# A two-layer transformer kernel: the opening on a turned copy of x, token-form first gates with the norm's root applied late, and the last block's last unit in two column halves

## The chip, the cores and the metric

One core of one Trainium2 chip. The metric is the device time of one launch in microseconds, lower is better; the number compared is the median of several runs.

## The reference

Batch 1, 256 tokens, model width 1024, all fp32. Two stacks of two layers each run one after the other. What matters here is the very first sub-block and the very last one:

```python
h = x                                                   # 256 x 1024
h = h + 0.5 * swiglu(rmsnorm(h, ffn1_norm[0]), w_gate, w_up, w_down)   # D_FF = 2816
# rmsnorm(x, g) = x * rsqrt(mean(x*x) + 1e-6) * g ;  swiglu = (silu(u @ w_gate) * (u @ w_up)) @ w_down
u = rmsnorm(h, mix_norm[0]);  z = u @ w_in[0]           # the mixer: attention, pooling, gates ...
...                                                     # the rest of both stacks
# second stack, last layer: r = ALPHA * h + relu(h @ w_ff1)**2 @ w_ff2 ; out = layer_norm(r, ln2_g, ln2_b)
```

The root of an RMS norm is one number per token, the gain one number per column of x. So (x * root * g) @ W equals root * ((x * g) @ W), row by row.

## The kernel before, in words

**Products.** Every weight comes from HBM once, as a *unit* of at most 128x2048 fp32 (1 MB), into one of six buffers `raw` (NL = 6). ScalarE (ACT) copies it to a rounded high part `wh` (`high`, five buffers, NH = 5), VectorE (DVE) subtracts to get a low part `wl` (`low`). Activations are split the same way into `xh`/`xl` (slots X, 8 column blocks of 128) or `mh`/`ml` (slots M, 12). A product is three matmuls per block: low weight, high weight, and low activation with high weight.

- *Token form* (`group`, item `tokens`, L1529): the activation is stationary, 512 (or fewer) weight columns move. A unit is visited once for each 128 tokens, t = 0 and 1. The result has tokens on the partitions and must be turned (four 128x128 transposes on TensorE (PE), L1552, then ACT high and DVE low) before the down product can use it.
- *Wide form* (`wide_group`, item `wide`, L1540 and L1543): the weight is stationary, 8 matmuls of 512 and 8 of 256 columns for each 128 of a unit's 256 columns. The result is already turned; DVE adds its halves (`wadd`).

**The plan.** `Plan` writes one list of items, once, before any instruction exists; each engine's program walks it and issues its own part, so the list's order is each engine's queue order. After each visit (or each half of a wide group) `tick` runs: deferred items, then `pump`, then `advance`, which places `fetch` of unit j once unit j-6 is used up, and `high` of j once j-5 is (`low` of j follows at the next `advance`). `pump` resumes the head generator of each of four lanes once. A lane is a first-in first-out queue: what is appended to it starts only when the generator ahead has ended.

Lane 0 first holds `opening`. In the kernel before its first statements place the rest of the norm and the turning of x, `consts` comes at pump 8, and then `tables` follows:

```python
def tables(self):
    for _ in range(40):
        yield
    for i in range(10):
        self.add("table", i=i)
        yield
```

That is: table 0 at pump 48, table 9 at pump 57, lane 0 free from pump 58. After a sub-block's last down units, `after(t, b)` places the squares, at b = 1 also the norm (`rms`), and appends a generator for turning the normed h of these 128 tokens into slots X: to lane 0 for t = 0, to lane 3 for t = 1. It yields WAIT_RMS = 2 times and then places both turns. If a product finds its slots not ready, `need` pumps until the turn is placed, and then goes on with the product behind it.

**Layer 0, `ffn1`.** 2816 columns in two rounds, (512, 512, 512) and (512, 512, 256). The first 512 are in token form: gate in units of 2 blocks, up in units of 4 (6 units). All others are in wide form, 256 columns at a time. Each round ends with `down`: 6 units, then 5 (one, and four visited first all by t = 0, then all by t = 1, `end=True`). That makes 12 + 16 + 12 + 20 + 10 = 70 ticks; the last visit of t = 0 is followed by pump 66, that of t = 1 by pump 70. The mixer's first group starts with four visits of t = 0.

**The opening.** SP issues x of t = 0, two units, x of t = 1, then more units. PE runs filling matmuls (`wake`) and spreads the gain row over the partitions through PSUM (`spread`, L1563, waits for a 4 KB DMA issued by ACT). For t = 0: squares on ACT, root on GpSimd (POOL, power of -0.5), norm on DVE into `xn`, turn, split; then product; the rest and t = 1 are placed between the first visits. `held` keeps `advance` from placing splits meanwhile.

**The end.** The last `down` group visits four units (two 512-deep weight halves times two column halves b) by t = 0, then by t = 1. Per column half: `hadd` (L2026), `bn_stats` (L2041); after b = 1 `bn_aggr`, then POOL adds epsilon and takes the power (L1433, L1436) while DVE does (h - mean) * g (L2049), DVE finishes (L2055), SP stores.

Of the kernel before, what the change touches and what calls it, by code (L numbers as in the profile page):

```python
# [3 lines left out]

# [4 lines left out]
F32 = mybir.dt.float32  # L9
# [10 lines left out]
L = 2  # L20
# [46 lines left out]
class Memory:  # L67


    def __init__(self, nc, A, out, ctx):  # L70
# [20 lines left out]
        self.fill_set, self.first_set = s("fill_set"), s("first_set")  # L91
        self.rows_set, self.row_landed = s("rows_set"), s("row_landed")
# [28 lines left out]
                      "weights_ready": self.weights_ready, "y_low": self.y_low}  # L121
# [11 lines left out]
    def sbuf(self):  # L133
# [36 lines left out]
        self.lam = A("lam", take(8), [P, 2])  # L170
        self.bn = A("bn", take(128), [P, 2, 16])
# [21 lines left out]
        self.gain_rows = A("gain_rows", o_g[0], [P, D])  # L193
        self.fill = A("fill", o_g[0] + 4096, [P, 512], F32R)
        self.first = A("first", o_g[0] + 6144, [P, P])
# [164 lines left out]
class Plan:  # L360
# [5 lines left out]
    def __init__(self, total):  # L366
# [9 lines left out]
        self.held = False  # L376
# [119 lines left out]
    def group(self, jobs, start=False, end=False):  # L496

        idx = [self.take(j["key"]) for j in jobs]
        for t, u in self.visits(len(jobs), start, end):
# [8 lines left out]
            v = self.pe("tokens", j=j, t=t, X=X, slots=slots, segs=segs, first=job["first"], stop=job["last"], need=need)  # L508
# [7 lines left out]
            if job["last"]:  # L516
                job["epi"](t, v["p"], [u[0] for u in segs])
# [35 lines left out]
    def once_open(self, go):  # L553

        def gen():
            while self.held:
                yield
            for _ in range(8):
                yield
            go()  # L560
        if self.held:
            self.lanes[3].append(gen())
        else:
            go()
# [7 lines left out]
    def rms(self, t, gain, final=False, halves=(0, 1)):  # L572
        n = self.next("normed", 2)
        self.add("rms", t=t, gain=gain, final=final, sq=self.count["squared"], n=n, c=self.next("rstd"), halves=halves,
                 spread=self.spread if gain == 0 else None)
# [5 lines left out]
    def rms_rest(self, t, gain):  # L581
        self.add("rms", t=t, gain=gain, final=False, c=self.count["rstd"] - 1, halves=(1,),
                 spread=self.spread)
# [28 lines left out]
    def to_ln(self, gname, bname, l, last=False):  # L612
        g, b_ = self.gain_load(gname, l), self.gain_load(bname, l)

        def after(t, b):
            self.add("stats", t=t, b=b, need=self.h_half[t, b])
            if b:
                n = self.next("normed", 2)
                self.add("ln", t=t, g=g, b=b_, n=n, c=self.next("rstd"), m=self.next("mean"))
# [11 lines left out]
    def down(self, name, l, k0, n_units, sizes, coef, after):  # L631
# [4 lines left out]
        def half_epi(b):  # L636
# [3 lines left out]
            return f  # L640
        u = 0
        for size in sizes:
            first, last = u == 0, u + size == n_units
            if last and after:
                self.group([dict(key=(name, (l,), k0 + (2 * u + 4 * i) * P, 4, 512 * b, 512), X="M",
                                 slots=[2 * u + 4 * i + k for k in range(4)], segs=[(b, 0, 512)],
                                 first=first and i == 0, last=(i == size // 2 - 1), epi=half_epi(b))
# [14 lines left out]
    def ffn1(self, l, pre, after, loads):  # L662
        self.mix_to_ffn()
# [3 lines left out]
        for n0, chunks, sizes in ((0, (512, 512, 512), (2, 4)), (1536, (512, 512, 256), (1, 4))):  # L667
            self.clear("M", range(12))
            slot, c0 = 0, n0
            for n in chunks:  # L670
                if c0 > 0:
# [5 lines left out]
                else:  # L677
                    kt = {gate: 2 if len(self.units) == 0 else 4, up: 4}
                    self.group([dict(key=(name, (l,), k * P, kt[name], c0, n), X="X",
                                     slots=list(range(k, k + kt[name])), segs=[(b, 0, n)], first=(k == 0),  # L680
                                     last=(k + kt[name] == 8), epi=self.silu_t if b == 0 else self.up_t(slot))
                                for b, name in ((0, gate), (1, up)) for k in range(0, 8, kt[name])], start=True)
# [4 lines left out]
    def silu_f(self, i, p, use):  # L687
        self.add("silu", i=i, p=p, use=use, free=self.sg_free[i])
        self.sg_use[i] = use

    def silu_t(self, t, p, uses):
        self.silu_f(t, p, uses[0])

    def upmul(self, i, p, use):
        self.add("upmul", i=i, p=p, use=use, sg=self.sg_use[i], free=self.mn_free[i])
        self.sg_free[i] = ("evac", use)
# [26 lines left out]
    def up_t(self, slot):  # L723
        def epi(t, p, uses):
            self.upmul(t, p, uses[0])
            self.later_turn(t, slot, uses[0])
        return epi
# [26 lines left out]
    def later_turn(self, t, slot, use):  # L754
        def go():
            if self.due[t] is go:
                self.due[t] = None
                p = self.turn("M", slot, t, ("mn", t), 4, [("evac", use)], max(self.m_free[slot + i] for i in range(4)))
# [23 lines left out]
    def ffn2(self, l, after, loads):  # L782
# [3 lines left out]
        for n0, n_chunks, sizes in ((0, 3, (2, 4)), (1536, 2, (2, 2)), (2560, 3, (2, 4))):  # L786
# [13 lines left out]
            self.down("w_ff2_2", l, n0, n_chunks * 2, sizes, 1.0, after if n0 == 2560 else None)  # L800


    def start(self):
        self.sg_use = {}
        self.h_ready = {t: [("x_landed", t)] for t in range(2)}
        self.h_half = {(t, b): ("x_landed", t) for t in range(2) for b in range(2)}
        g = 0
        self.gain_n = 1
        self.add("load", t=0)
        self.add("fetch", j=0, after=None)  # L810
        self.add("fetch", j=1, after=None)
        self.add("load", t=1)
        self.fetched = 2
        self.held = True
        self.advance()
        self.pe("wake", n=4)
        v = self.pe("spread")
        self.pe("wake", n=3)
        self.spread = v["p"]
        self.x_free, self.x_war = -1, None  # L820
        for b in range(2):
            self.square(0, b)
        ready = self.rms(0, g, halves=(0,))
        self.split_next()
        self.turn("X", 0, 0, ("xn", 0, 0), 4, [ready[0]])
        self.pe("wake", n=4)
        self.rms_rest(0, g)
        self.split_next()
        for b in range(2):
            self.square(1, b)  # L830
        self.lanes[0].append(self.opening(g, ready))

    def opening(self, g, ready):

        self.turn("X", 4, 0, ("xn", 0, 1), 4, [ready[1]])
        self.split_next()
        yield
        ready = self.rms(1, g, halves=(0,))
        self.split_next()
        self.rms_rest(1, g)  # L840
        yield
        self.turn("X", 0, 1, ("xn", 1, 0), 4, [ready[0]])
        yield
        self.turn("X", 4, 1, ("xn", 1, 1), 4, [ready[1]])
        self.held = False
        for _ in range(4):
            yield
        self.add("consts")
        yield from self.tables()
# [558 lines left out]
def sp_program(e, m, plan):  # L1408

    sp = Engine(e, m, None)  # L1410
    for it in plan.items:
# [6 lines left out]
        elif k == "load":  # L1418
            t = it["t"]
            e.dma_start(m.h[:, t, :], m.A["x"][0, t * P:t * P + P, :]).then_inc(m.x_landed[t], 16)  # L1420
        elif k == "store":
# [6 lines left out]
def pool_program(e, m, plan):  # L1428
# [9 lines left out]
    for it in plan.items:  # L1438
# [6 lines left out]
        elif k == "rms" and 0 in it["halves"]:  # L1445
# [7 lines left out]
            e.tensor_tensor(rs, rs, m.nhalf[:, :], ALU.pow).then_inc(m.rstd_ready, 1)  # L1453
        elif k == "ln":
# [3 lines left out]
        elif k == "load" and it["t"] == 0:  # L1458
            e.memset(m.gain_rows[:, :], 0.0).then_inc(m.rows_set, 1)
# [49 lines left out]
def pe_program(e, m, plan):  # L1509
# [4 lines left out]
    for it in plan.items:  # L1514
# [39 lines left out]
        elif k == "wake":  # L1554
            pe.wait_ge(m.fill_set, 1)
            for c in range(it["n"]):
                ins = e.matmul(pb[7][:, :], m.fill[:, 0:P], m.fill[:, :], start=True, stop=True)
            ins.then_inc(m.pe_done, 1)
        elif k == "spread":
            pe.wait_ge(m.first_set, 1)  # L1560
            pe.wait_ge(m.row_landed, 16)
            for q in range(2):
                ins = e.matmul(pb[1 + 2 * q][:, :], m.first[:, :], m.gain_rows[:, 512 * q:512 * q + 512], start=True, stop=True)  # L1563
# [192 lines left out]
def act_program(e, m, plan):  # L1756
# [4 lines left out]
    for it in plan.items:  # L1761
# [3 lines left out]
        if k == "load" and t == 0:  # L1765
            e.dma_start(m.ident[:, :], m.A["c_ident"]).then_inc(m.ident_landed, 16)
            a.wait_ge(m.rows_set, 1)
# [600 lines left out]
```

## Time and profile before

| | us |
|---|---|
| median of 3 runs (2071.65 to 2072.18) | 2071.84 |
| the profiled execution: its own time | 2072.52 |
| its span, first to last instruction | 2070.7 |
| PE busy in the span | 2054.7 |
| DVE busy | 1407.6 |
| ACT busy | 1013.6 |
| mean DMA rate | 181 GB/s |

The span begins with the first instruction of any engine and ends with the last; the profiled execution took 1.8 us more than its span. Busy PE time counts overlapping, modelled ends, so pace (start to start) says more than duration. "Idle before, releaser" names the instruction or transfer that ended a wait. The chain of waits follows the work that ended last, back to the start.

### The profile page before, as it was taken

What the parts mean: (1) busy time and instruction counts of PE and PEld (TensorE: products, weight loads), DVE (VectorE), ACT (ScalarE), POOL (GpSimd) and SP (SyncE); (2) the same over time, 40 slices, a digit from 0 to 9 for tenths busy, and PEclk for the clock granted to TensorE, in tenths of its full rate; (3) what the DMA queues carried; (4) which work ended last, traced back from release to release, by engine and by line L of the source; (5) the groups of instructions that cost most, each with busy time, mean ns of one, the idle gap of its engine ahead of it and who ended that gap; (6) DMA issues with size and microseconds to landing.
All of it is one profiled execution on the core that took longest, in us unless ns stands there. A gap on an engine that the chain in (4) does not pass through costs nothing.

```text
span 2070.7 us, 25612 instructions
## 1 busy us (share of the span) xinstructions
PE 2054.7 (99%) x10571; PEld 1736.3 (84%) x10571; DVE 1407.6 (68%) x1664; ACT 1013.6 (49%) x1261; POOL 90.6 (4%) x123
## 2 busy tenths in 40 slices
PE   8999999999999999999999999999999999999998
PEld 6888888888888888888888888888888888888887
DVE  6676687676757566877676566657767667667675
ACT  5445486454444335675543455644544466444431
POOL 1000100000000001000100000010100000100000
PEclk9999999999999999999999999999999999999999
DMA  8665444475556556544655564544655645455552
GB/s 267 214 197 180 158 164 141 143 230 184 192 188 224 184 175 198 163 142 143 214 194 189 166 226 143 163 160 171 232 186 195 207 140 175 157 176 191 193 193 81
DMA packets 233334, 374.68 MB, mean 181 GB/s; under 512 B 8466, under 2 KB 129426, under 8 KB 233219
## 3 DMA queue, kind: packets, MB, share of 16 engines
q1 hardware_dynamic: 229408, 360.60, 53.0%
q0 software_dynamic: 3664, 12.38, 2.1%
q8 instruction: 84, 1.38, 0.3%
q14 instruction: 32, 0.25, 0.0%
q10 hardware_dynamic: 146, 0.07, 0.0%
HBM read 371.97 MB, written 1.05 MB: 180 GB/s over the span
## 4 chain that ended last, share of the span: by engine, by line
PE 98%; DVE 1%; ACT 0%; DMA 0%; issue 0%; POOL 0%; POOLq 0%; DVEq 0%
PE pb L1529 58%; PE pb L1540 21%; PE pb L1543 11%; PE pb L1552 2%; PE pb L1603 1%; PE pb L1674 1%; PE pb L1673 0%; DVE wl L1986 0%; PE pb L1611 0%; PE pb L1612 0%; PE pb L1737 0%; PE pb L1610 0%; PE pb L1661 0%; ACT wh L1774 0%; DMA gain_rows<-in_ffn_norm_dram 0%; PE pb L1696 0%
## 5 line engine op out<-in xcount | busy, mean ns | idle before, releaser
L1774 ACT ACTIVATE wh<-raw 128x2048 fp32r<-128x2048 f32 (+3 forms) x348 | 656.5, 1887 | 669.2 <-PE pb L1529 276.5
L1986 DVE TENSOR_TENSOR wl<-raw,wh 128x2048 fp32r<-128x2048 f32 (+3 forms) x348 | 780.3, 2247 | 165.4 <-ACT wh L1774 164.9
L1529 PE MATMUL pb<-wh,x 128*128 128x512 f32 x1856 | 571.0, 389 | 0.0
L1540 PE MATMUL pb<-x,wh 128*128 128x512 f32 x1856 | 468.2, 394 | 0.0
L1529 PEld LDWEIGHTS pb<-wh,x 128*128 128x128 f32 x1856 | 348.8, 188 | 68.7
L1540 PEld LDWEIGHTS pb<-x,wh 128*128 128x128 f32 x1856 | 335.0, 189 | 61.6 <-issue 0.7
L1529 PE MATMUL pb<-wl,x 128*128 128x512 f32 x928 | 370.4, 399 | 2.0 <-DVE wl L1986 1.5
L1543 PEld LDWEIGHTS pb<-x,wl 128*128 128x128 f32 x1856 | 253.2, 190 | 18.3
L1543 PE MATMUL pb<-x,wl 128*128 128x256 f32 x1856 | 258.7, 282 | 0.0
L1529 PE MATMUL pb<-wl,mh 128*128 128x512 f32 x736 | 254.6, 392 | 0.0
L1529 PE MATMUL pb<-wh,ml 128*128 128x512 f32 x736 | 252.9, 389 | 0.0
L1529 PE MATMUL pb<-wh,mh 128*128 128x512 f32 x736 | 252.7, 389 | 0.0
L1529 PEld LDWEIGHTS pb<-wl,x 128*128 128x128 f32 x928 | 174.4, 188 | 40.1 <-issue 4.3
L1529 PEld LDWEIGHTS pb<-wh,ml 128*128 128x128 f32 x736 | 138.2, 188 | 29.1
L1529 PEld LDWEIGHTS pb<-wh,mh 128*128 128x128 f32 x736 | 138.2, 188 | 28.4
L1529 PEld LDWEIGHTS pb<-wl,mh 128*128 128x128 f32 x736 | 137.3, 188 | 27.1
L2000 DVE TENSOR_REDUCE sg<-pb 128x256 f32<-128x512 f32 x120 | 82.3, 686 | 44.0 <-PE pb L1543 43.9
L2026 DVE SCALAR_TENSOR_TENSOR h<-pb,h 128x512 f32<-128x512 f32 x72 | 48.0, 685 | 87.9 <-PE pb L1529 87.9
L2000 DVE TENSOR_REDUCE mn<-pb 128x256 f32<-128x512 f32 x72 | 49.4, 686 | 62.4 <-PE pb L1543 62.3
L1529 PE MATMUL pb<-wl,yph 128*128 128x512 f32 x128 | 51.3, 401 | 0.0
L1529 PE MATMUL pb<-wh,ypl 128*128 128x512 f32 x128 | 50.0, 390 | 0.0
L1529 PE MATMUL pb<-wh,yph 128*128 128x512 f32 x128 | 49.9, 390 | 0.0
(354 smaller groups left out, 1560.6 us busy)
## 6 DMA issues: line engine op xcount, KB each, us to landing
raw<-in_w_in_dram SPq DMA_DIRECT2D x100, 1024.0 KB, 5.3
raw<-in_w_ff_dram SPq DMA_DIRECT2D x64, 1024.0 KB, 5.2
raw<-in_ffn_w_up_dram SPq DMA_DIRECT2D x44, 1024.0 KB, 5.4
raw<-in_ffn_w_down_dram SPq DMA_DIRECT2D x44, 1024.0 KB, 5.0
raw<-in_ffn_w_gate_dram SPq DMA_DIRECT2D x42, 1024.0 KB, 5.3
raw<-in_w_branch_dram SPq DMA_DIRECT2D x24, 1024.0 KB, 5.0
raw<-in_w_out_dram SPq DMA_DIRECT2D x16, 1024.0 KB, 5.0
raw<-in_w_in_dram SPq DMA_DIRECT2D x4, 832.0 KB, 4.5
```

What stands on the lines that cost most here:

```text
L1529: ins = e.matmul(pb[b][:, 0:c1 - c0], x[:, s, cols], w[:, n, c0:c1], start=(it["first"] and n == 0 and q == 0), stop=(it["stop"] and n == ...
L1540: e.matmul(bank[:, :], hi[:, s, c], m.x2[:, s, :, :].rearrange("p a s -> p (a s)"), start=(s == 0), stop=False, skip_group_check=True)
L1543: ins = e.matmul(bank[:, 0:S], lo[:, s, c], m.xh[:, s, :], start=False, stop=(s == 7), skip_group_check=True)
L1552: ins = e.transpose(bank[:, c * P:c * P + P], m.tile(it["src"], c), ident[:, :])
L1603: ins = e.transpose(bank[:, c * P:c * P + P], Sb[:, c * P:c * P + P], ident[:, :])
L1674: e.matmul(bank[:, 128:384], Q[0:w, P:S], key, start=True, stop=True).then_inc(m.pe_done, 1)
L1774: e.activation(hi, raw, ACT.Copy).then_inc(m.high_done, 1)
L1986: e.tensor_tensor(lo, raw, hi.bitcast(F32), ALU.subtract).then_inc(m.low_done, 1)
L2000: e.tensor_reduce(m.half(it["dst"], i), bank[:, :].rearrange("p (a s) -> p s a", a=2), AXX, ALU.add).then_inc(m.evac[use[0]], 1)
L2026: e.scalar_tensor_tensor(o, bank[:, :], it["coef"], o, ALU.mult, ALU.add).then_inc(m.evac[use[0]], 1)
```

## The change

1. **x turned.** The host also passes x transposed (`xT`) and the first gain as a column (`gcol`). SP loads two blocks of `xT`, units 0 and 1, the other six blocks, units 2 to 5, and only then x itself. ACT scales each block by the gain into `xh`, DVE makes `xl`. No turn of x, no norm and no `spread` in the opening.
2. **The root goes late.** `root` (squares on ACT, power on POOL) is placed after 6 visits; `silu` takes it as its scale and `upmul` as its scalar. This needs tokens on the partitions, so *all* gate and up columns of layer 0's `ffn1` are now in token form. Units of the first 512 columns: gate 1, 1, 2, 2, 2 blocks, up 2, 2, 4; visits alternate t = 0, 1.
3. **Lane 0.** `opening` yields 5 times, places squares and roots, yields 16 times, then `consts` and the unchanged `tables`.
4. **The end.** For t = 1 the last unit is done as two 256-column products in banks of their own, each with its own add and statistics (`hcut`); the partial sum of the unit before it is added on its own. `lnend` adds epsilon on DVE; POOL only takes the power.

```diff
@@ group
+            done = job["last"] or (t == 1 and job.get("sum", False))
+            if t == 1 and job.get("cut"):
+                for q in range(2):
+                    use = self.side()
+                    v = self.pe("tokens", j=j, t=t, X=X, slots=slots, segs=[(use, 256 * q, 256 * q + 256)], first=True,
+                                stop=True, need=need)
+                    job["cut"](q, v["p"], use)
...
@@ ffn1
+        opening = not self.units
...
-                if c0 > 0:
+                if c0 > 0 and not opening:
...
+                    parts = {gate: (4, 4), up: (4, 4)}
+                    if opening and c0 == 0:
+                        parts = {gate: (1, 1, 2, 2, 2), up: (2, 2, 4)}
+                    elif n == 256:
+                        parts = {gate: (8,), up: (8,)}
...
+                                for k, kt in zip(accumulate((0,) + parts[name]), parts[name])], start=not opening)
...
+    def silu_t(self, n, root):
+        def epi(t, p, uses):
+            while root and len(self.roots) < 2:
+                self.pump()
+            self.add("silu", i=t, p=p, use=uses[0], free=self.sg_free[t], n=n, root=root)
...
@@ start
+        self.add("load_turned", i=0)
+        for j in range(NL):
+            self.add("fetch", j=j, after=None)
+            if j == 1:
+                self.add("load_turned", i=1)
+        for t in range(2):
+            self.add("load", t=t)
...
+        self.pe("wake", n=9)
+        self.x_free = -1
+        for slots in ((0,), (1,), (2, 3), (4, 5), (6, 7)):
+            for s in slots:
+                self.add("xsplit", slot=s)
+                for t in range(2):
+                    self.ready["X", s, t] = ("x_low", s + 1)
+            self.split_next()
+        self.lanes[0].append(self.opening())
+
+    def opening(self):
+
+        for _ in range(5):
             yield
+        for t in range(2):
+            for b in range(2):
+                self.square(t, b)
+            self.add("root", t=t, sq=self.count["squared"])
+            self.roots.append(self.next("rstd"))
+        for _ in range(16):
+            yield
+        self.early = False
         self.add("consts")
         yield from self.tables()
@@ act_program
+        elif k == "xsplit":
+            s = it["slot"]
+            a.wait_ge(m.col_landed, 16)
+            a.wait_ge(m.xt_landed[s > 1], 16)
+            e.activation(m.xh[:, s, :], m.xT[:, s, :], ACT.Copy, scale=m.gcol[:, s:s + 1]).then_inc(m.x_high, 1)
@@ dve_program
+        elif k == "hcut":
...
+            v.step(e.scalar_tensor_tensor(o, bank[:, 0:256], it["coef"], o, ALU.mult, ALU.add))
+            v.own_steps()
+            v.step(e.bn_stats(m.bnl[:, 6 * q:6 * q + 6], o))
```

## Rows read from the trace of the kernel before

**Rows 1.** The page's chain that ended last: shares of the span by engine.

```profile
PE 98%; DVE 1%; ACT 0%; DMA 0%; issue 0%; POOL 0%; POOLq 0%; DVEq 0%
```

**Rows 2.** Windows: length, busy us (instructions) by engine, PE clock, DMA share, GB/s.

```profile
8.00:10.00 2.00, 2.00 (x4) 0.97 (x3) 0.00 (x0) 0.00 (x0) 0.00 (x0) 1.00 1.04 391
...
30.00:35.00 5.00, 5.00 (x24) 4.13 (x23) 2.94 (x2) 3.58 (x3) 0.00 (x0) 1.00 1.10 349
```

**Rows 3.** Instructions on tile h up to 30 us: issue to landing of x's two loads.

```profile
DMA to landing us min/median/max: 4.0/5.2/6.5
```

**Rows 4.** Timeline of the opening: start us, us, engine, line, what, [idle before].

```profile
2.14 0.47 SPq L1420 DMA_DIRECT2D h<-in_x_dram  x1
...
6.08 1.06 ACT L1774 ACTIVATE wh<-raw 128x1024 fp32r<-128x1024 f32 x1
...
6.16 3.75 PE L1563 MATMUL pb<-gain_rows,first 128*128 128x512 f32 x4 [2.65 <-DMA gain_rows<-in_ffn_norm_dram]
...
10.69 1.22 DVE L1986 TENSOR_TENSOR wl<-raw,wh 128x1024 fp32r<-128x1024 f32 x1
...
13.52 0.62 ACT L1804 ACTIVATE xn<-h 128x512 f32<-128x512 f32 x1
```

**Rows 5.** Chain of waits up to 60 us: start us, us, what.

```profile
1.71 4.32 DMA gain_rows<-in_ffn_norm_dram
...
9.91 1.28 PE pb L1557 x3
...
18.52 1.66 PE pb L1529 x6
...
20.61 1.39 PE pb L1529 x6
...
39.01 1.81 PE pb L1540 x8
...
44.57 0.44 PE pb L1552 x4
45.01 1.85 PE pb L1540 x8
46.85 0.95 PE pb L1543 x8
```

**Rows 6.** Timeline where layer 0's `ffn1` ends and the mixer begins.

```profile
200.81 0.39 PE L1529 MATMUL pb<-wh,ml 128*128 128x512 f32 x1
...
201.27 1.92 ACT L1774 ACTIVATE wh<-raw 128x2048 fp32r<-128x2048 f32 x1 [0.85 <-DMA raw<-in_w_in_dram]
...
201.77 0.68 DVE L2026 SCALAR_TENSOR_TENSOR h<-pb,h 128x512 f32<-128x512 f32 x1
...
203.09 0.61 ACT L1804 ACTIVATE xn<-h 128x512 f32<-128x512 f32 x1
...
204.27 0.56 POOL L1453 TENSOR_TENSOR st<-st,nhalf 128x1 f32<-128x1 f32 x1
...
204.87 1.42 DVE L2036 SCALAR_TENSOR_TENSOR xn<-h,st,gain 128x512 f32<-128x512 f32 x2 [2.41 <-POOL st L1453]
...
206.20 4.49 DVE L1986 TENSOR_TENSOR wl<-raw,wh 128x2048 fp32r<-128x2048 f32 x2
...
210.60 1.28 DVE L2021 TENSOR_TENSOR x<-pb,x 128x512 fp32r<-128x512 f32 x2
```

**Rows 7.** Chain of waits from 2050 us to the end.

```profile
2049.99 13.16 PE pb L1529 x58
...
2063.18 0.70 DVE h L2026
...
2064.93 0.78 POOL bn L1433
...
2065.75 0.97 POOLq L2328
...
2066.81 0.75 DVE h L2055
```

More of the change, by code:

```diff
@@ L615, in after @@
         def after(t, b):
-            self.add("stats", t=t, b=b, need=self.h_half[t, b])
+            end = last and t == 1
+            if not (end and b):
+                self.add("stats", t=t, b=b, need=self.h_half[t, b], end=end)
             if b:
                 n = self.next("normed", 2)
-                self.add("ln", t=t, g=g, b=b_, n=n, c=self.next("rstd"), m=self.next("mean"))
+                self.add("lnend" if end else "ln", t=t, g=g, b=b_, n=n, c=self.next("rstd"), m=self.next("mean"))
                 self.gain_user = [n + 2, n + 2]
@@ L628, in to_ln, with down @@
         return after
-    def down(self, name, l, k0, n_units, sizes, coef, after):
+    def down(self, name, l, k0, n_units, sizes, coef, after, end=False):
         def epi(t, p, uses):
@@ L640, in half_epi, with add_up, cut @@
             return f
+        def add_up(t, p, uses):
+            self.hadd(t, 1, p, uses[0], coef)
+            if t == 0:
+                after(0, 1)
+        def cut(q, p, use):
+            self.add("hcut", t=1, q=q, p=p, use=use, coef=coef, need=self.h_ready[1])
+            if q:
+                after(1, 1)
         u = 0
@@ L677, in ffn1 @@
                 else:
[L678 to L682, printed above, removed]
+                    parts = {gate: (4, 4), up: (4, 4)}
[3 more added lines that the diff above has]
+                        parts = {gate: (8,), up: (8,)}
+                    self.group([dict(key=(name, (l,), k * P, kt, c0, n), X="X", slots=list(range(k, k + kt)),
+                                     segs=[(b, 0, n)], first=(k == 0), last=(k + kt == 8),
+                                     epi=self.silu_t(n, opening) if b == 0 else self.up_t(slot, n, opening))
+                                for b, name in ((0, gate), (1, up))
+                                for k, kt in zip(accumulate((0,) + parts[name]), parts[name])], start=not opening)
                 slot += n // P
@@ L808, in start @@
         self.gain_n = 1
[L809 to L823, printed above, removed]
@@ L1444, in pool_program @@
             e.dma_start(m.gain[n % 2][:, :], vec.partition_broadcast(P)).then_inc(m.gain_landed[n % 2], 16)
-        elif k == "rms" and 0 in it["halves"]:
+        elif k in ("rms", "root"):
             t = it["t"]
@@ L1556, in pe_program @@
             for c in range(it["n"]):
[L1557 to L1563, printed above, removed]
+                ins = e.matmul(pb[7][:, :], m.fill[:, :], m.fill[:, :].unsqueeze(1).broadcast_to([P, 4, P]), start=True,
+                               stop=True)
             ins.then_inc(m.pe_done, 1)
```

169 lines of the change are left out of this document (95 added, 74 removed).

## The prediction, made before the changed kernel was run

> **What bounds it now.** First the page's chain by engine: PE holds 98% of it [rows 1], so only four places can matter: where PE does not yet work on products, where it gets other work, where it would have to wait, and what follows its last matmul. Then the opening's chain: the products of the first 512 columns end at 39.0 us, where the first wide matmul stands [rows 5]. Their own work is 16 blocks x 2 token halves x 3 matmuls. A token-form matmul takes 13.16/58 = 0.227 us [rows 7], so this is 96 x 0.227 = 21.8 us; 17.2 us are start, waits and turns. Then the tail behind PE: from 2063.2 to 2070.7 us [rows 7]. Last the border between `ffn1` and mixer, for the order of each queue there [rows 6]; the page shows nothing wrong at it, and it is where I expect most of the gain to go.
>
> **Part 1, the opening: 8.5 us less.** Landing: the second load of x was issued at 2.14 and took 6.5 us (the longer of the two) [rows 3, 4], with some 2.2 MB in the queue up to its end, so 2.2 MB have landed at 8.6. More come at 391 GB/s; rows of 1 KB, as `xT` has, at 349 [rows 2], which adds 0.3 us for it. In the new order unit 2 ends at 2.2 MB: 8.9; unit 3 10.3, unit 4 11.6, unit 5 13.0, x 15.7, unit 6 17.0, unit 7 (1 MB) 19.7. Feeding: `high` of 1024 columns takes 1.06 us, of 512 about 0.62, of 2048 1.92; `low` of 1024 takes 1.22, of 2048 2.25 [rows 4, 6]. By the same lines a 256-column piece of x costs ACT 0.40 and DVE 0.43.
> Units 0 and 1: `xT` and unit 0 land near 4.9; a piece of x, `high`, `low` give PE its first product near 6.2. The gain column must be there too: a 4 KB transfer issued by ACT took 4.32 us in the full queue [rows 5]; first in the queue it is there by 5, and even 2 us more would be hidden, since PE does units 0 and 1 in 2.7 us and then waits for unit 2. Unit 2: 8.9 + 1.06 + 1.22 = 11.2. From there PE has units 2 to 6, 10 blocks x 6 x 0.227 = 13.6 us, until 24.8. Their splits keep ahead (each adds at most 1.9 us of ACT or DVE to PE's 2.7). Unit 7: ACT does `high` of unit 6 until 18.1, then the four squares that the plan places ahead of unit 7 (4 x 0.67, to 20.7), `high` of unit 7 to 22.7, `low` to 24.9. So unit 7 starts at 24.9 and takes 5.4: end 30.4, against 39.0. ACT's `silu` waits come behind two more splits and hold nothing up. Bounds: with no waits at all behind 6.2 the end is 28.0 (gain 11); with each piece of x at the 512-column price (0.62 and 0.70, eight times) unit 2 and the splits behind it come up to 2.3 us later (gain 6).
>
> **Part 2, token form: 2.1 us more.** Half a wide group takes 1.85 + 0.95 = 2.80 us, so 512 columns of gate and up cost 8 x 2.80 = 22.4. In token form it is 96 x 0.227 = 21.8 plus two turns of 0.44 [rows 5]: 22.7. Four such chunks: +1.2. The 256-column chunk: 4 x 2.80 = 11.2 before; after, 96 matmuls of 256 columns at 0.95/8 = 0.119 [rows 5], 11.4, and two half turns, some 0.5: +0.8. In sum about 2.1; bounds 1.2 (turns wholly inside the pace) and 3.5 (the last products wait for a turn). DVE loses its `wadd` work, which was hidden and is worth nothing. The six buffers cover the fetches; 1 MB per 5.4 us is below 349 GB/s.
>
> **Part 3, the end: 0.75 us less.** After the last matmul stand add 0.70, statistics 0.70, aggregate, POOL 0.78 and 0.97, then DVE [rows 7]. With 256 columns add and statistics take 0.43 each: -0.55. POOL's first step goes to DVE as a tiny one, but DVE's two 0.7 steps (h - mean) now end behind the power, not before it: only about 0.35 is left of 0.78. 24 matmuls of 0.119 for 12 of 0.227 add 0.15. Bounds 0.3 and 1.2.
>
> **Part 4, lane 0: 7.2 us more.** Nothing of this is in the diff's new lines; it follows from the count of ticks. After the change `opening` yields at pumps 1 to 5 and 6 to 21, `consts` comes at 22, table 0 at 62, table 9 at 71, and the lane is free from 73. `ffn1` has 16 + 8 + 8 + 12 + 20 + 10 = 74 ticks, 4 more than before, while the tables come 14 later. The last visit of t = 0 ends with tick 70: the turn of the mixer's first input is appended behind tables 8 and 9, yields at 73 and 74 and is placed at 75, which is behind all visits of t = 1. Before, it came two visits ahead of the end. The mixer begins with t = 0, so PE finds `need` unmet, turns, and waits for the split. Queue order then: on ACT square, `high`, turn; on DVE the add for t = 1, the *norm of t = 1*, a `low`, and only then the low part of t = 0's turn. Let T = 201.0 be the end of the last visit [rows 6]. Add at 201.8 (behind a `low`), square 203.1 (behind a `high`), power to 204.8, norm 204.9 to 206.3, `low` 2.25 to 208.5 ([rows 6] has two in 4.49; one stands before this turn), low part of the first half turn (half of 1.28) to 209.1 = T + 8.1. Before, PE went on at T; of the 8.1, 0.9 is the turning itself, which it had paid earlier. Net 7.2. Bounds: 2 if the norm of t = 1 and the `low` were out of the way (only turn, high and low of the split), 9.5 with the second `low` ahead too [rows 6]. I take 7.2, since the queue orders are fixed by the plan. Nothing gives it back: PE has no idle time behind it to shrink.
>
> **The clock: 2 us more.** The trace's clock column reads 1.00 at 8 to 10 us [rows 2], but from 9.9 on three 512-column matmuls took 1.28 us, 0.427 each [rows 5], the pace of 1.2 GHz; at 20.6 they take 0.23, that of 2.4 GHz. The slow stretch began after a gap of 2.65 us [rows 4] and lasted from 6.2 to 11.2 at least, costing half of it, 2.5 to 2.8 us. The gap before 18.5 (PE had last turned x) cost no pace [rows 5]. A new gap of 7.2 us, with only two turns ahead, is longer than either; I take 2.0, ends 0 and 2.8. The Trainium skill (TensorE: Matmul & The Clock Gate, "What's actually happening") says that the lower clock is the default and comes back once the array idles; by it this loss is certain, and the gap before unit 2 is a risk too. No row of this trace shows a warm array cooling down.
>
> **Sum.** -8.5 + 2.1 - 0.75 + 7.2 + 2.0 = +2.05, on the profiled execution 2072.5 + 2.05 = 2074.6 (its span is 1.8 shorter). The median of the runs lies 0.7 below the profiled one: 2073.9. About 0.2%, 4.1 us, is what a measurement can tell from no change here; the forecast is inside it.
>
> **Rivals.**
> *The turn is not late (faster).* If the lane is free in time, or the late placing costs only what ACT and DVE need for the turn, parts 4 and clock fall away: -7.15, so 2064.7. For it: the chain shows no wait there now, and the change is local to the opening. Against: the pump counts. Chance 0.12.
> *The clock decides (slower).* PE comes to unit 2 at 11.2 after a gap of 2.3 us, much like the 2.65 that preceded the slow stretch. If the array is then at 1.2 GHz for 5 us, as at 6.2 to 11.2, that costs 2.6 more in the opening; with 2.8 at the border the sum is +5.5: 2077.3. It decides as soon as the pace behind 11.2 is 0.43 and no longer 0.23. Against it: nine filling matmuls and units 0 and 1 keep PE at work to 8.9, and the 18.5 gap did no harm. Chance 0.18. That page's rule is this rival's mechanism.
> *The opening gives nothing.* The first products still wait, for x's squares, since `silu` needs the root and ACT's queue is in order: the end of the first columns then is near 36, and the sum +7.6: 2079.5. Against: unit 7 is the only split behind the squares. Chance 0.06.
> Forecast 0.58, other small mixes 0.06 to either side.
>
> **Range.** The forecast's own spread, from the bounds of the opening (2.5 either way), the border (7.2 down to 5.5 or up to 9) and the clock, is 2070.5 to 2077.5. To hold 8 in 10 I give 2069 to 2079: it leaves out the faster rival and the far end of the third. Faster by over 0.2%: the first rival and a little of the forecast, 0.13. Slower by over 0.2% (over 2076.0): the two slower rivals, and an eighth of the forecast's own, 0.31. Within: 0.56.
>
> **What would show it.** First products near 6, unit 2 near 11, first token matmul of the second 512 columns near 30 to 31. Some 22.7 us per 512-column chunk. At the border, near 195 us: PE idle for some 7 us behind two turns of xn, released by DVE's turn (the low part), with the norm of t = 1 and one `low` between on DVE; table instructions of DVE in the visits just before. Then 0.43 per matmul for a few us. Last matmul to end 0.9 shorter. I am wrong if PE has no gap at the border, or if the time between 10 and 30 us has waits of more than 3 us.

## The result: 0.3% slower, and the profile after

| | before | after |
|---|---|---|
| median of the runs compared (us) | 2071.66 (8 runs, 2071.03 to 2072.18) | 2077.61 (8 runs, 2076.56 to 2080.48) |
| ratio, 95% interval | | 1.003 (1.0021 to 1.0039) |
| profiled execution, its span (us) | 2072.5, 2070.7 | 2078.7, 2076.9 |
| the changed kernel's forecast (us) | | 2073.9, range 2069 to 2079 |

The change costs 5.95 us. That is inside the range and 3.7 us above the forecast; 0.29% is more than the 0.2% that counts as no change here, so the case given 0.31 came true and not the one given 0.56.

The page's chain of waits is where to begin, as before [rows 1]. DMA has gained 2%, ACT and DVE show up too; PE's share has fallen.

```profile
PE 95%; DMA 2%; DVE 2%; ACT 1%; issue 0%; SPq 0%; POOL 0%; DVEq 0%
```

PE's waits of the changed kernel over the whole run (engine, line, released by: total us, times, longest):

```profile
PE pb L1558 <- DVE wl L2018: 10.7, 3, 7.2
...
PE pb L1558 <- DVE h L2063: 1.0, 1, 1.0
...
PE pb L1581 <- DVE mn L2025: 0.3, 1, 0.3
```

The first line is three waits, one of them of 7.2 us. The chain up to 60 us (start us, us, what), against [rows 5], shows what the opening waited for, and one more wait behind it, at 41 us:

```profile
2.69 8.10 DMA raw<-in_ffn_w_gate_dram
...
10.81 1.07 ACT wh L1802
...
11.90 1.24 DVE wl L2018
...
24.41 12.07 DMA raw<-in_ffn_w_up_dram
...
40.66 0.76 DVE mn L2025
...
41.47 0.66 PE pb L1581 x4
```

Unit 2 (the first unit of two blocks, 1024 columns in all), issued at 2.69 us, lands 8.10 us later, at 10.8; its `high` and `low` give PE its product at 13.18. A unit of the up weights, issued at 24.41 us, takes 12.07 us to land. The timeline of the opening (start us, us, engine, line, what, [idle before]), against [rows 4]:

```profile
3.91 1.28 ACT L1796 ACT_TABLE_LOAD   x1 [3.91 <-DMA xT<-in_xT_dram]
...
5.21 0.51 ACT L1796 ACTIVATE x<-xT,gcol 128x256 fp32r<-128x256 f32 x1
...
7.01 0.79 PE L1558 MATMUL pb<-wl,x 128*128 128x512 f32 x1 [1.83 <-DVE wl L2018]
...
8.46 0.63 PE L1558 MATMUL pb<-wl,x 128*128 128x512 f32 x1
...
9.74 0.61 PE L1558 MATMUL pb<-wl,x 128*128 128x512 f32 x1
...
13.18 0.50 PE L1558 MATMUL pb<-wl,x 128*128 128x512 f32 x1 [1.66 <-DVE wl L2018]
```

Windows of the opening (as in [rows 2]; the last two columns are DMA share and GB/s):

```profile
4.00:5.00 1.00, 1.00 (x3) 0.37 (x2) 0.00 (x0) 1.00 (x1) 0.00 (x0) 1.00 0.82 292
5.00:6.00 1.00, 0.19 (x1) 0.00 (x0) 0.25 (x1) 0.99 (x3) 0.00 (x0) 1.00 0.77 134
6.00:7.00 1.00, 0.00 (x0) 0.00 (x0) 0.96 (x3) 1.00 (x3) 0.00 (x0) 1.00 0.94 285
```

The border between `ffn1` and mixer, against [rows 6]:

```profile
190.93 0.15 DVE L2161 TENSOR_TENSOR lam<-epsc 128x1 f32<-128x1 f32 x1
...
197.76 1.03 PE L1581 MATMUL pb<-ident,xn 128*128 128x128 f32 x8
199.15 0.68 DVE L2063 SCALAR_TENSOR_TENSOR h<-pb,h 128x512 f32<-128x512 f32 x1
...
201.66 1.41 DVE L2070 SCALAR_TENSOR_TENSOR xn<-h,st,gain 128x512 f32<-128x512 f32 x2 [1.83 <-POOL st L1478]
...
203.00 2.29 DVE L2018 TENSOR_TENSOR wl<-raw,wh 128x2048 fp32r<-128x2048 f32 x1
205.20 1.28 DVE L2058 TENSOR_TENSOR x<-pb,x 128x512 fp32r<-128x512 f32 x2
205.98 0.69 PE L1558 MATMUL pb<-wl,x 128*128 128x416 f32 x1 [7.19 <-DVE wl L2018]
206.47 0.90 PE L1558 MATMUL pb<-wh,x 128*128 128x416 f32 x2
...
211.99 0.55 PE L1558 MATMUL pb<-wh,x 128*128 128x416 f32 x2
```

The two half turns of the mixer's first input are the last thing that PE does before it stands still, and their low part stands on DVE behind the norm of t = 1 and a `low`. The view names `wl` as the releaser of the wait, but L2018 ended 0.7 us before PE went on; what came last was the first half of L2058. Two matmuls then take 0.90 us, and later 0.55: the first ones run at the slow pace. The granted clock agrees (windows as above; the last three columns are PE clock, DMA share and GB/s): it is 0.53 here, near the lower of its two levels, 1.2 GHz.

```profile
206.00:212.00 6.00, 6.00 (x22) 5.70 (x23) 0.48 (x1) 0.60 (x2) 0.00 (x0) 0.53 0.00 0
```

The end of the chain, against [rows 7]:

```profile
2049.95 20.34 PE pb L1558 x101
...
2070.31 0.44 DVE h L2085
...
2073.04 0.75 DVE h L2102
```

**The account of the two profiled executions**, in the prediction's parts:

| part | predicted (us) | read (us) | from |
|---|---|---|---|
| opening: start of the next 512 columns | -8.5 | -6.6 | 39.01 to 32.38 |
| token form, up to the last visit | +2.1 | +4.3 | 32.38 to 197.76 is 165.4; before, 39.01 to 201.03 less the turns' 0.9 is 161.1 |
| border: turn placed late | +7.2 | +7.3 | T to T + 8.2, less 0.9 |
| slow pace behind it | +2.0 | +2.4 | from the last visit to the mixer's first wide matmul 32.2 (197.76 to 229.94), before 21.6 (201.03 to 222.64); less the turns' 0.9 and the gap's 7.3 |
| end | -0.75 | -0.8 | 7.5 to 6.6, and 0.15 more of PE |
| sum | +2.05 | +6.5 | the spans differ by 6.2; the other 0.3 lies between 230 us and the last matmul and isn't explained |

### The profile page after: what moved, and what is told of

The parts are those of the page before. It is cut to its first block, busy times and chain, and to the rows that moved or that the text cites. A ratio compares the mean times of both kernels' runs of the same rounds, so it can differ in the third digit from the quotient of the medians.

```text
span 2076.9 us, 25431 instructions
## 1 busy us (share of the span) xinstructions
PE 2055.0 (99%) x10501; PEld 1736.2 (84%) x10501; DVE 1385.9 (67%) x1634; ACT 1012.5 (49%) x1267; POOL 85.6 (4%) x122
## 4 chain that ended last, share of the span: by engine, by line
PE 95%; DMA 2%; DVE 2%; ACT 1%; issue 0%; SPq 0%; POOL 0%; DVEq 0%
PE pb L1558 61%; PE pb L1569 17%; PE pb L1572 9%; PE pb L1581 2%; DMA raw<-in_ffn_w_up_dram 1%; PE pb L1627 1%; ACT wh L1802 1%; PE pb L1698 1%; DVE wl L2018 0%; DMA raw<-in_ffn_w_gate_dram 0%; PE pb L1697 0%; PE pb L1635 0%; PE pb L1636 0%; DMA raw<-in_w_in_dram 0%; PE pb L1761 0%
## 5 line engine op out<-in xcount | busy, mean ns | idle before, releaser
L2018 DVE TENSOR_TENSOR wl<-raw,wh 128x2048 fp32r<-128x2048 f32 (+3 forms) x350 | 780.9, 2236 | 175.8 <-ACT wh L1802 175.3
L1558 PE MATMUL pb<-wh,x 128*128 128x512 f32 (+2 forms) x2176 | 664.0, 387 | 0.0
L1558 PEld LDWEIGHTS pb<-wh,x 128*128 128x128 f32 x2176 | 408.8, 189 | 79.2
L1558 PE MATMUL pb<-wl,x 128*128 128x512 f32 (+2 forms) x1088 | 431.8, 397 | 11.7 <-DVE wl L2018 10.7
L1569 PE MATMUL pb<-x,wh 128*128 128x512 f32 x1568 | 396.0, 394 | 0.0
L1569 PEld LDWEIGHTS pb<-x,wh 128*128 128x128 f32 x1568 | 283.2, 189 | 52.1 <-issue 0.7
L1558 PE MATMUL pb<-wl,mh 128*128 128x512 f32 (+1 forms) x740 | 255.7, 391 | 0.0
L1558 PE MATMUL pb<-wh,ml 128*128 128x512 f32 (+1 forms) x740 | 253.8, 389 | 0.0
L1558 PE MATMUL pb<-wh,mh 128*128 128x512 f32 (+1 forms) x740 | 253.6, 388 | 0.0
L1572 PEld LDWEIGHTS pb<-x,wl 128*128 128x128 f32 x1568 | 213.9, 190 | 15.4
L1572 PE MATMUL pb<-x,wl 128*128 128x256 f32 x1568 | 218.6, 282 | 0.0
L2058 DVE TENSOR_TENSOR ml<-pb,mh 128x512 fp32r<-128x512 f32 (+1 forms) x42 | 28.0, 675 | 35.5 <-ACT mh L1829 35.5
```

Source lines behind the costliest of these rows:

```text
L1558: ins = e.matmul(pb[b][:, 0:c1 - c0], x[:, s, cols], w[:, n, c0:c1], start=(it["first"] and n == 0 and q == 0), stop=(it["stop"] and n == ...
L1569: e.matmul(bank[:, :], hi[:, s, c], m.x2[:, s, :, :].rearrange("p a s -> p (a s)"), start=(s == 0), stop=False, skip_group_check=True)
L1572: ins = e.matmul(bank[:, 0:S], lo[:, s, c], m.xh[:, s, :], start=False, stop=(s == 7), skip_group_check=True)
L2018: e.tensor_tensor(lo, raw, hi.bitcast(F32), ALU.subtract).then_inc(m.low_done, 1)
L2058: e.tensor_tensor(lo, src, hi.bitcast(F32), ALU.subtract).then_inc(m.evac[use[0]], 1)
```

## The experiments

The numbers are those of the expectations; there is no E8. All are timed in five rounds beside the kernel before: 2071.63 us in the first group (E1 to E4), 2071.95 in the second (E5, E6, E7, E9), 2071.86 in the third (E10 to E13). A difference is against that.

**E1: the tables early again.** The changed kernel with one number changed:

```
-        for _ in range(40):
+        for _ in range(20):
```

> The changed kernel with the tables' wait cut from 40 to 20 pumps, so that lane 0 is free long before the mixer's first input is to be turned; nothing else changes. Theory (the turn queued behind the tables): PE's 7.2 us gap at the border and the slow pace behind it go, 7.3 + 2.4 = 9.7 us less than the changed kernel, near 2068, and 3 to 4 us under the kernel before. Rival (the gap is the backlog of DVE: norm of t = 1 and splits, whoever is placed when): at most 1 us less, near 2077.

2068.68 us, ratio 0.9986 (0.9978 to 0.9995): 2.95 faster than before, 8.9 faster than the change. The border in its timeline:

```profile
192.87 1.03 PE L1581 MATMUL pb<-ident,xn 128*128 128x128 f32 x8
193.66 0.48 PE L1558 MATMUL pb<-wl,mh 128*128 128x512 f32 x1
...
199.20 0.35 PE L1558 MATMUL pb<-wl,x 128*128 128x416 f32 x1
199.39 0.54 PE L1558 MATMUL pb<-wh,x 128*128 128x416 f32 x2
```

The turn again stands among visits, there is no gap, and the pace is the fast one from the start. The tick at which the tables come, on which the mixer's first input doesn't depend, decides 9 us. Its profiled execution also has a slower opening than the change's (the next 512 columns start at 33.34 us, not 32.38), and lacks the wait at 41 us; with both, 9.7 becomes 9.2, and the spans differ by 9.1:

```profile
12.63 0.79 PE L1558 MATMUL pb<-wl,x 128*128 128x512 f32 x1 [2.78 <-DVE wl L2018]
...
14.07 0.63 PE L1558 MATMUL pb<-wl,x 128*128 128x512 f32 x1
...
15.35 0.63 PE L1558 MATMUL pb<-wl,x 128*128 128x512 f32 x1
...
16.34 0.39 PE L1558 MATMUL pb<-wl,x 128*128 128x512 f32 x1
```

A token-form block (three matmuls) takes 0.68 us at the fast pace and 1.28 at the slow one. Behind a pause of 2.78 us three blocks go slowly; the granted clock from 14 to 17 us is 0.67, and in the change 1.00. The edit touches nothing there. Units 0 and 1 ran fast from 6.83 us in this execution and slowly, until about 10 us, in the change's, so this pause was the longer one.

**E2: the kernel before with the tables late.** The cause without the change:

```
-        for _ in range(40):
+        for _ in range(50):
```

> The kernel before with the tables' wait raised from 40 to 50 pumps: lane 0 is free from pump 68, and the first turn for the mixer is placed at pump 71, behind all visits, as in the changed kernel. Theory (late turn alone makes gap and slow pace): 9.7 us more than the kernel before, near 2081.4, with a PE gap of some 7 us at the border. Rival (the changed opening or token form is needed for it): under 2 us more.

2080.69 us, ratio 1.0041 (1.0029 to 1.0054): 9.1 slower. Its timeline has the change's border:

```profile
198.85 1.03 PE L1552 MATMUL pb<-ident,xn 128*128 128x128 f32 x8
206.79 0.69 PE L1529 MATMUL pb<-wl,x 128*128 128x416 f32 x1 [6.91 <-DVE wl L1986]
```

With E1 this shows part 4 from both sides: the late tick makes the gap in the kernel before, and without it the changed kernel has none.

**E3: the gap filled.** The changed kernel, with 28 matmuls of 512 columns into a free bank behind the two half turns (their result is used by nothing), so that PE waits at work:

```
+            if half and t == 0 and not self.filled:
+                self.filled = True
+                self.pe("keep", n=28, g=self.gen[0])
...
```

> The changed kernel with 28 matmuls of 512 columns that nobody reads, placed behind the two late half turns, so that PE works through 6.4 of the 7.2 us of its gap. Theory (the slow pace is the lower clock that follows idling): the products behind the gap keep 0.19 us per 416 columns, 2.4 us less than the changed kernel, near 2075.2. Rival (the slow pace has another cause there, or the filler delays the splits): no gain, 2077 or more.

2075.46 us, ratio 1.0019 (1.001 to 1.0028): 2.15 faster than the change, with the gap as long as it was. Its timeline:

```profile
197.68 6.61 PE L1595 MATMUL pb<-mh 128*128 128x512 f32 x28
205.06 0.43 PE L1561 MATMUL pb<-wl,x 128*128 128x416 f32 x1 [0.78 <-DVE x L2067]
205.33 0.54 PE L1561 MATMUL pb<-wh,x 128*128 128x416 f32 x2
```

and the window behind it:

```profile
206.00:212.00 6.00, 6.00 (x36) 5.63 (x35) 3.32 (x3) 1.91 (x7) 0.39 (x1) 1.00 0.01 3
```

Two 416-column matmuls take 0.54 at once, against 0.90, and the granted clock is 1.00, against 0.53. So the slow pace is the lower clock, it belongs to PE's idleness and is worth 2.15 us by the times and 2.4 by the account. This view also names the true releaser of the wait, L2067, DVE's low part of the turn.

**E4: the token form alone.** The kernel before, with all of layer 0's `ffn1` columns in token form (its opening, end and ticks as they were):

```
-                if c0 > 0:
+                if c0 > 0 and not opening:
...
+                               start=not opening or c0 == 0)
```

> The kernel before, old opening, with all gate and up columns of layer 0's first sub-block in token form. Theory (token form itself costs 2.1 us by pace and turns, and its first visit of t = 1 in round 2 waits 1.4 us for the bank that the down product left): 3.5 to 4.4 us more than before, near 2075.5. Rival (the waits came from the changed opening's late weights): 2.1 us more, 2073.8.

2073.92 us, ratio 1.0011 (1.0002 to 1.002): 2.3 slower. The price of the form is the one predicted (2.1), and the 4.3 of the account, which I had by then taken for the form's own price, is not. PE's waits of this kernel have neither the wait for `h` nor the one for `mn` that the changed kernel has; most of the rest of the 4.3 is those two. E4's second round starts in the same order as the change's (in layer 0's `ffn1` the last line of its edit is true for the first 512 columns alone), and still there is no wait for `h`: DVE's addition ends at 119.1 us there and PE wants the bank at 119.64. What differs is the `low` ahead of it, and behind that the weights. In the change GpSimd's loads for the mixer, one of them 768 KB, are issued from 98.7 to 101.6 us (first line), in E4 and in the kernel before at 64 to 68 us (E4: third line):

```profile
99.81 0.54 POOL L1505 DMA_DIRECT2D pc<-in_c_pool_dram  x1
...
110.88 1.92 ACT L1802 ACTIVATE wh<-raw 128x2048 fp32r<-128x2048 f32 x1 [7.71 <-DMA raw<-in_ffn_w_up_dram]
...
64.91 0.55 POOL L1481 DMA_DIRECT2D pc<-in_c_pool_dram  x1
```

The unit of up weights issued at 101.2 us takes 9.7 us to land, where its neighbours take 4.9 to 5.0, and from 102 to 104 us all queues together move 47 GB/s. The place of these loads is again a matter of ticks: a lane places them a fixed count of pumps after `opening` has opened it, which the changed kernel does only at pump 22. That they delay the unit is read from these times; no run moved them alone.

**E5: without the new end.** E1 with the last block in one piece:

```
-            end = last and t == 1
+            end = False
...
```

> The kernel with the early tables (near 2068.7) and the end of the kernel before: last unit of t = 1 in one piece, its add and statistics on 512 columns, epsilon on GpSimd. Theory (the split end is worth 0.8 us): near 2069.5. Rival (the 24 short matmuls and DVE's steps give the gain back): no difference.

2069.55 us, ratio 0.9989 (0.998 to 0.9998): 2.4 faster than before, where E1 is 2.95. The end is worth 0.55 by that and 0.8 by the chain. The intervals are wider than either, so by the times alone it is not settled.

**E6: longer rows for x.** E1 with `xT` laid out as [128, 8, 512] in memory, so that its rows are 2 and 6 KB and not 1:

```
-    a["xT"] = g["x"][0].T
+    a["xT"] = g["x"][0].T.reshape(8, P, S).transpose(1, 0, 2)
...
```

> The kernel with the early tables, with the turned x laid out by the host so that each partition's part is one piece of 2 KB and one of 6 KB instead of pieces of 1 KB. Theory (the short pieces lowered the DMA rate between 4 and 8 us and so made unit 2 land 1.9 us late): unit 2 splits near 9.5 instead of 10.3 to 10.8, 1 to 1.5 us less, near 2067.4. Rival (the number of small transfers in flight at the start lowers it, whatever the rows): under 0.4 us less.

2068.30 us, ratio 0.9983 (0.9974 to 0.9991): 3.65 faster than before, 0.7 better than E1, which is no more than its spread. The windows of this kernel say why it is neither nothing nor much:

```profile
4.00:5.00 1.00, 1.00 (x3) 0.38 (x2) 0.00 (x0) 0.22 (x1) 0.00 (x0) 1.00 1.02 356
5.00:6.00 1.00, 0.19 (x1) 0.00 (x0) 0.00 (x0) 1.00 (x1) 0.00 (x0) 1.00 1.14 457
```

From 4 to 7 us the queue runs at 356 to 457 GB/s, where the change had 134 to 292: the short rows of `xT` slowed it. Unit 2 lands at 9.6 us (9.5 in E11), and at 10.8, 10.2, 10.3, 10.6 and 10.4 in the profiles of the change, E1, E3, E5 and E7, whose openings are the same. But the first piece of x lands at 4.8 and not at 3.6 to 4.0, the first product comes at 7.9 and not near 7, and PE runs at the slow pace until about 13.5.

**E7: the second round first.** In the changed kernel `ffn1`'s second round in layer 0 starts without the reordering that the old token form had; a bank that t = 1 needs is then freed by an addition behind a `low`. E1 with

```
-                                for k, kt in zip(accumulate((0,) + parts[name]), parts[name])], start=not opening)
+                                for k, kt in zip(accumulate((0,) + parts[name]), parts[name])],
+                               start=not opening or c0 == n0 > 0)
```

> The kernel with the early tables, with the first group of round 2 visited four times by t = 0 before t = 1 comes. Theory (t = 1's first visit waits 1.1 to 1.4 us for the bank that DVE's add of the down product still holds): that wait goes, 1.2 us less, near 2067.5. Rival (the wait only moves, since the splits behind are as late): no difference.

2066.76 us, ratio 0.9974 (0.9964 to 0.9984): 5.2 faster than before and 2.2 better than E1. The row of the change that it takes away is the second of these, in the timeline of the changed kernel:

```profile
115.04 1.28 DVE L2063 SCALAR_TENSOR_TENSOR h<-pb,h 128x512 f32<-128x512 f32 x2
...
115.78 0.50 PE L1558 MATMUL pb<-wl,x 128*128 128x512 f32 x1 [1.02 <-DVE h L2063]
```

E7's list of PE's waits has no such line, though the unit lands as late (ACT's `high` at 111.09 us): the new order hides the delay. The wait for `h` costs 1.2 to 1.3 us in the change, and this is all that the edit explains. The rest is the opening, which it doesn't touch: in E7's profiled execution the pause before unit 2 is 1.58 us with the fast pace behind it, where E1's has 2.78 and the slow one, and the next 512 columns start at 31.94 us and not 33.34; a wait for `mn` of 0.9 us, which E1 has not, takes part of that back. 1.4 - 0.9 + 1.2 is the 1.7 us by which the two spans differ.

**E9: the activation table early.** E1, with a one-column copy on ACT ahead of its first real work, so that the table load of 1.28 us is over before x lands:

```
+            a.wait_ge(m.half_set, 1)
+            e.activation(m.lam[:, 0:1], m.nhalf[:, :], ACT.Copy)
```

> The kernel with the early tables and one copy of a single column placed on ACT ahead of its first waits, so that the 1.28 us table load runs before x has landed. Theory (the opening is bound by the landing of unit 2): the first product starts 1.3 us earlier, near 5.6, and unit 2 no earlier; under 0.4 us less in total. Rival (each us of the first start counts): 1.3 us less, near 2067.4.

2070.15 us, ratio 0.999 (0.9982 to 0.9999): 1.8 faster than before, but 1.1 worse than E1. Its timeline:

```profile
5.85 0.50 PE L1558 MATMUL pb<-wl,x 128*128 128x512 f32 x1 [0.66 <-DVE wl L2020]
...
12.85 0.79 PE L1558 MATMUL pb<-wl,x 128*128 128x512 f32 x1 [3.35 <-DVE wl L2020]
```

The first product comes 1.2 us sooner than in the change, and unit 2 hardly (12.85 against 13.18; 12.63 in E1): so the pause before it grows to 3.35 us, and the slow pace stands behind it. In E1's profiled execution it stands there too, and the spans are 2067.6 and 2067.8 us; the 1.1 is less than the spread of either kernel's runs (3.3 and 3.5), so no gain is seen, and a loss isn't shown.

**E10: the four together.** The changed kernel with the edits of E1, E6, E7 and E9, no new one:

```
+E1 range(20)   +E6 long rows   +E7 start of round two   +E9 early table
```

> Early tables, long rows of the turned x, round 2 started by t = 0, and the early table load together. Theory (with long rows PE no longer waits between units 1 and 2, so an earlier first product now counts, and the array has no pause to slow down behind): 2.2 us for round 2, 0.7 for the rows and 1.3 for the first product below the kernel with the early tables: near 2064.8. Rival (the first product is then bound by the landing of the first turned blocks): near 2066.

2066.49 us, ratio 0.9975 (0.9965 to 0.9985): 5.4 faster than before, the fastest of all, 0.2 from E7 and so not to be told from it. Unit 2 now comes at 12.02 us behind a pause of 0.50. The 1.3 us expected of an earlier first product aren't there: it comes at 7.06 us, no sooner than in the change, since ACT's first piece of x starts only at 5.05, released by the landing of the gain column, although the table load was over by 2.9; and units 0 and 1 run slowly until about 10 us.

**E11: more filling ahead.** E10 with 13 filling matmuls at the start for 9:

```
-        self.pe("wake", n=9)
+        self.pe("wake", n=13)
```

> The same with 13 filling matmuls in place of 9, so that PE is at work until its first product. Theory (without a pause ahead of the first product the pace reaches 0.23 us earlier): 1 to 1.5 us less than with 9 fillers, near 2063.5. Rival (it takes its time from the start whatever is added, or the fillers delay the first product): no gain.

2066.79 us, ratio 0.9977 (0.9968 to 0.9986): no gain. Units 0 and 1 run fast from 6.98 us on, and unit 2 still comes at 11.93: it waits for its landing.

**E12: the first block of x by itself.** E11 with `xT`'s first two blocks in two loads:

```
-            a, b = ((0, 2), (2, 8))[it["i"]]
+            a, b = ((0, 1), (1, 2), (2, 8))[it["i"]]
...
```

> The same as with 13 fillers, with the first two turned blocks loaded each by itself, the second behind unit 0. Theory (the first product waits for 256 KB where it needs 128): first product 0.5 us earlier, 0.3 to 0.5 us less. Rival (a further transfer costs SP's queue as much as it saves, since every later unit moves back): no gain or a loss of up to 0.5 us.

2068.93 us, ratio 0.9987 (0.9979 to 0.9996): 2.9 faster than before, and 2.1 worse than E11. The first product is at 6.33 us, and

```profile
12.93 0.80 PE L1559 MATMUL pb<-wl,x 128*128 128x512 f32 x1 [3.68 <-DVE wl L2021]
```

unit 2 comes 1.0 us later than in E11 (with one more transfer ahead of it, it is issued 0.5 us later and takes 0.5 us longer), after a pause of 3.68 us, at the slow pace.

**E13: more filling in E1.** E1 with 14 filling matmuls:

```
-        self.pe("wake", n=9)
+        self.pe("wake", n=14)
```

> The kernel with the early tables and 14 filling matmuls in place of 9. Theory (a pause between units 1 and 2 near 2.8 us lets the array fall back to the low pace, and PE's earlier work does not help): no gain, near 2068.7 or up to 1 us more, since units 0 and 1 run faster and the pause grows. Rival (the slow stretch behind 12.6 us comes from too little work ahead of the first product): 1.5 us less, near 2067.2.

2069.59 us, ratio 0.9988 (0.9979 to 0.9997): 2.3 faster than before, no gain on E1. In its timeline unit 2 comes behind a pause of 2.91 us:

```profile
12.85 0.50 PE L1558 MATMUL pb<-wl,x 128*128 128x512 f32 x1 [2.91 <-DVE wl L2018]
13.65 0.50 PE L1558 MATMUL pb<-wl,x 128*128 128x512 f32 x1
...
14.80 0.63 PE L1558 MATMUL pb<-wl,x 128*128 128x512 f32 x1
```

The first block behind the pause is still fast (0.80 us); from 13.65 us the blocks take 1.15 to 1.28 us until 17.3, and the granted clock from 14 to 17 us is 0.50. Filling ahead of the first products doesn't help where the pause comes after them.

## Why the prediction was right in its shape and 3.7 us short

**The border (part 4) was right** to 0.1 us, in place, order and length: tables in the visits just before, two half turns, then the norm of t = 1 and one `low` on DVE ahead of the low part. E1 and E2 show that the count of ticks causes it. This is the part that turns a gain into a loss: without it the same change is 2.95 us faster (E1).

**The clock (2.0) was right**: 2.4 by the account, 2.15 by E3. No row of before showed a warm array slowing; E3 shows it, since with the same time lost but PE at work the pace and the granted clock (1.00 against 0.53) are kept. The Trainium skill (TensorE: Matmul & The Clock Gate, "What's actually happening") says that the low clock is the default and comes back once the array idles; the trace agrees at the border (7.2 us) and, in E1, E9, E12 and E13, behind pauses of 2.8 to 3.7 us; behind 1.6 to 1.9 us (E7, the change, E11) the fast pace stayed.

**The opening (part 1) was over-sized by 1.9 us.** The step that failed is "in the new order unit 2 ends at 2.2 MB: 8.9". I took 391 GB/s and 0.3 us for the short rows; in the windows from 4 to 7 us the queue moved 292, 134 and 285 GB/s, and unit 2 landed at 10.8. The splits behind it took 2.4 us with their hand-overs, as forecast (2.3). The first product came at 7.01 and not 6.2, since ACT's table load (1.28 us) began only once x had landed. That was forgotten, and was hidden: PE waited for unit 2 anyway, and E9, which takes it away, gained nothing. E6 shows that the rows of `xT` were a part of it: with long rows unit 2 lands 0.6 to 1.2 us sooner, at 9.6, which still is 0.7 us behind 8.9, and that was not taken apart. From unit 2 on the order held: no wait between 13.18 and 32.38 us, 19.2 us for 28 blocks, as forecast (11.2 to 30.4).

**The token form (part 2) was right in its price, 2.1 against 2.3 in E4, and missed two waits.** "The last products wait for a turn" stood in the bounds and not in the sum. What failed is "the six buffers cover the fetches", a term put at nothing: it compared mean rates, and both waits stand behind a unit that landed late, 12.1 us and 9.7 us after its issue. At 41.47 us the turn of t = 1 waits for DVE's product, which stands behind a `low` whose weights had only just landed: 0.5 us, the distance of the two turns being 3.65 us there and 3.19 in E4. At 115.78 us the first product of t = 1 waits for its bank, 1.2 to 1.3 us. This second one needs two things: a detail of the diff that I read past, `start=not opening`, which takes the reordering away from the second round too (E7 gives it back), and the late landing, which stands beside GpSimd's loads, moved there by ticks; E4 has the first without the second, and no wait.

**The end (part 3) was right**: 0.8 by the chain; the times can't tell it (E5).

**The sum.** Of the 4.5 us by which the account exceeds the forecast, 1.9 are the landing of unit 2, 2.2 the token form (1.7 of it the two waits) and 0.4 the pace. Each part's bounds held what was read but for the token form (4.3 against 3.5 at most); the two misses had one sign, and together they are as large as the no-change bound.

**The rivals.** "The turn is not late" fell with E2 and the timeline. "The opening gives nothing" fell: it gives 6.6. "The clock decides" named a total near the one measured (2077.3) with a mechanism that was not at work in the profiled execution: PE's pause before unit 2 was 1.66 us there and the pace behind it fast. But the mechanism is real: it stands in the openings of E1, E9, E12 and E13. The runs of the changed kernel spread over 3.9 us and those of the kernel before over 1.2; a pause that is sometimes on the one side and sometimes on the other would do that. For it: the change, E1, E3, E5 and E7 have the same opening, and in their profiles the next 512 columns start at 32.38, 33.34, 32.17, 32.16 and 31.94 us, latest in the one with the pause of 2.78; and the longest run of the change (2080.48 us) has the lowest mean granted clock (0.995, the others 0.996 or 0.997). Against it: E3's and E7's runs spread over 1.4 and 1.6 us only. It stays open.

**The version to keep** is E10 or E7: 2066.5 to 2066.8 us, some 0.25% faster than the kernel before. What still bounds E10's opening is the landing of unit 2, and behind it that of a unit of up weights at 35.45 us, 12.2 us after its issue.

## What to carry to other kernels

Where a kernel's order comes from a plan that counts ticks, an edit at one end moves work at the other: recount every lane that is filled by ticks, up to the next place where an engine's order is strict, before believing a local gain. In an opening, ask which transfer the engine waits for last; work that only starts sooner makes the pause before it longer, which gained nothing in E9 and E13, and in E12, where the landing came later as well, cost 2.1 us. When a diff narrows a condition (`start=`), go through every caller that it used to be true for.

## What the runs showed of the hardware

- A warm TensorE fell to half its pace behind pauses of 2.78 (E1), 2.91 (E13), 3.35 (E9), 3.68 (E12), 6.91 (E2) and 7.19 us (the change), and kept it behind 1.58 (E7), 1.66 (the change) and 1.93 us (E11). The slow stretch lasted some 3 to 5.5 us. The profile's granted clock shows these stretches: 0.67, 0.50, 0.68 and 0.64 from 14 to 17 us in E1, E13, E9 and E12, 0.53 from 206 to 212 us in the change, and 1.00 there in E3, where filling matmuls took the gap's place. It doesn't show the first stretch after the start: from 7 to 10 us of the change it reads 1.00, while the blocks stand 1.28 us apart.
- From 4 to 7 us, with 1 KB rows in the queue, it moved 134 to 292 GB/s in the change (194 to 326 in E1, E3, E5 and E7), where the kernel before had 397 to 420 and E6, with 2 and 6 KB rows, 356 to 457. With the longer rows the first 256 KB of x landed 0.8 to 1.1 us later (4.8 us against 3.6 to 4.0), the queue moving 186 GB/s from 3 to 4 us against 362 to 385.
- ACT's table load (1.28 us) isn't issued ahead of time: it began when the first activation's semaphores were met (3.91 us). The Trainium skill (ScalarE: Activation LUTs, "What ACT_TABLE_LOAD costs") gives 1283 ns for the load and a drain of about 1380 ns for every switch of set; the first agrees, and of the second the trace shows nothing here: the activation began 0.02 us behind the load, and at a later load, at 188.53 us, 0.02 us lie before it and 0.02 behind.
